# Third block's mixing: one inverse root for four layer norms, and the first two heads' tiles among the fill

## Time and profile before

| what | us |
|---|---|
| median of three runs | 3507.39 |
| lowest and highest | 3506.89, 3510.99 |
| the profiled execution: its time | 3505.32 |
| its span, first to last instruction | 3503.5 |
| TensorE busy | 3274.1 (93%) |
| VectorE, ScalarE, GpSimd busy | 1465.8, 1016.5, 1149.7 |

### The profile page before, as it was taken

How to read it: one execution, slowest core, us unless ns; L and a number is a source line. 1 busy time by engine, 2 the same in 40 slices (tenths; PEclk the granted TensorE clock), 3 DMA queues, 4 the chain that set the end, 5 groups by cost and what they waited for, 6 DMA issues and landing times.

```text
span 3503.5 us, 41394 instructions
## 1 busy us (share of the span) xinstructions
PE 3274.1 (93%) x17274; PEld 2674.5 (76%) x17274; DVE 1465.8 (42%) x3149; ACT 1016.5 (29%) x1613; POOL 1149.7 (33%) x542
## 2 busy tenths in 40 slices
PE   5988999999999998999999989999987999899999
PEld 4767888887777786877777767888765777678887
DVE  4876656453211103646765342111127666431110
ACT  2232222223222222323313332222234334322221
POOL 2312333233333342312313323444331223334443
PEclk9988999999999998998999979999988999899999
DMA  2211112112233331101101212233321112222232
GB/s 91 84 43 49 46 46 67 49 49 78 85 119 121 123 95 50 49 19 49 49 19 61 73 49 72 97 98 95 91 79 37 52 64 73 66 65 98 96 98 89
DMA packets 71482, 247.92 MB, mean 71 GB/s; under 512 B 8064, under 2 KB 8448, under 8 KB 71168
## 3 DMA queue, kind: packets, MB, share of 16 engines
q1 hardware_dynamic: 71296, 245.28, 21.9%
HBM read 243.15 MB, written 2.10 MB: 70 GB/s over the span
## 4 chain that ended last, share of the span: by engine, by line
PE 83%; DVE 12%; ACT 3%; issue 1%; POOL 1%; DMA 0%; SPq 0%; DVEq 0%; ACTq 0%
PE bank L858 21%; PE bank L860 20%; PE bank L859 20%; PE bank L898 6%; PE bank L869 3%; PE bank L1121 1%; PE bank L876 1%; PE bank L892 1%; PE bank L1306 1%; PE bank L1324 1%; PE bank L883 1%; PE bank L1315 1%; DVE t L1494 1%; PE bank L1152 1%; DVE t L1430 1%
## 5 line engine op out<-in xcount | busy, mean ns | idle before, releaser
L2533 POOL TENSOR_TENSOR R<-W,R 128x1024 fp32r<-128x1024 f32 (+2 forms) x448 | 1041.3, 2328 | 2078.4 <-ACT R L2173 2078.4
L858 PE MATMUL bank<-u,R 128*128 128x512 f32 (+1 forms) x3440 | 1399.5, 407 | 50.8 <-issue 21.7
L859 PE MATMUL bank<-u,R 128*128 128x512 f32 (+1 forms) x3440 | 1358.8, 395 | 0.0
L860 PE MATMUL bank<-u,R 128*128 128x512 f32 (+1 forms) x3440 | 1358.3, 395 | 0.0
L858 PEld LDWEIGHTS bank<-u,R 128*128 128x128 f32 (+1 forms) x3440 | 656.8, 191 | 214.1 <-issue 53.6
L860 PEld LDWEIGHTS bank<-u,R 128*128 128x128 f32 (+1 forms) x3440 | 655.1, 190 | 145.1 <-issue 1.0
L859 PEld LDWEIGHTS bank<-u,R 128*128 128x128 f32 (+1 forms) x3440 | 657.1, 191 | 130.7 <-issue 4.0
L2173 ACT ACTIVATE R<-W 128x1024 fp32r<-128x1024 f32 (+2 forms) x448 | 451.0, 1013 | 197.9 <-PE bank L860 196.2
L898 PE MATMUL bank<-t,t 128*128 128x128 f32 x2000 | 242.2, 278 | 8.5 <-DVE t L1638 4.8
L898 PEld LDWEIGHTS bank<-t,t 128*128 128x128 f32 x2000 | 235.5, 193 | 15.5 <-DVE t L1638 5.5
L2190 ACT ACTIVATE u<-t 128x512 fp32r<-128x512 f32 x126 | 76.2, 626 | 351.1 <-DVE t L1464 304.7
(11 more groups left out here) (354 smaller groups left out, 2720.6 us busy)
## 6 DMA issues: line engine op xcount, KB each, us to landing
W<-in_in SPq DMA_DIRECT2D x48, 512.0 KB, 3.5
W<-in_ff_in SPq DMA_DIRECT2D x44, 512.0 KB, 3.4
W<-in_g_qkv SPq DMA_DIRECT2D x24, 512.0 KB, 3.4
W<-in_ada SPq DMA_DIRECT2D x24, 512.0 KB, 3.4
W<-in_f1g SPq DMA_DIRECT2D x22, 512.0 KB, 3.4
W<-in_f1u SPq DMA_DIRECT2D x22, 512.0 KB, 3.4
W<-in_f2g SPq DMA_DIRECT2D x22, 512.0 KB, 3.4
W<-in_f2u SPq DMA_DIRECT2D x22, 512.0 KB, 3.5
```

The lines of the kernel that those rows point to most:

```text
L858: e.matmul(b[0:cols, :], wh, hi, start=(k == 0), stop=False)
L859: e.matmul(b[0:cols, :], wh, lo, start=False, stop=False)
L860: i = e.matmul(b[0:cols, :], wl, hi, start=False, stop=(k == KT - 1))
L2533: e.tensor_tensor(R[q % NH][:, 1024:1024 + n], W[p % NW][:, 0:n], R[q % NH][:, 0:n].bitcast(F32), SUB).then_inc(*PN.pool.up("lo", key))
```

## The change

The six tiles of heads 0 and 1 no longer stand in the order ahead of the merge but head the first fill. The MLP's chain is no longer `gn 0, gn2 0, gn 1, gn2 1, ...` but four `gn`, one new step `gnn`, then four `gn2`. `gnn` waits for all four squares and computes the four inverse roots at once, on 128x4. The planner's costs are set anew to match.

```
 SMALL
-  gm0=6, gm1=6, gm2=6, gm3=6,
+  gm=24,
 SEG
-    gn="v1.63 s.81", gn2="v5.26", gs="p.88 v1.38"
+    gn="v1.33 s.81", gnn="v2.4", gn2="v1.4", gs="p.88 v1.38"
 order()
     O += [s for j in range(4) for s in tiles("in3", 20 + j, ("gv", j), ("gvt", j))]
-    O += attention_in(("f", 0)) + attention_in(("f", 1))
-    mlp = [x for m in range(4) for x in (("gn", m), ("gn2", m))]
+    mlp = [("gn", m) for m in range(4)] + [("gnn",)] + [("gn2", m) for m in range(4)]
     for f in range(4):
         mlp += [tiles("in3", 16 + f, ("gu", f)), ("gs", f), ("pair", "yg", f)]
...
     O += merge([[s for h in range(a, 8, 2) for s in diff_head(h)] for a in range(2)] + [mlp],
-               sum([attention_in(("f", h)) for h in range(2, 8)], []), rest)
+               sum([attention_in(("f", h)) for h in range(8)], []), rest)
 VectorE
             def gn(m):
-                c, x, sq_ = small["gm%d" % m], t(G_VT[m]), t(G_T[m % 3])
+                c, x, sq_ = small["gm"][:, m:m + 1], t(G_VT[m]), t(G_T[m % 3])
...
+            def gnn():
+                c = small["gm"]
+                w.wait_ge(*GM.act.at("var", 3))
+                e.tensor_scalar(c[:, 8:12], c[:, 4:8], 1.0 / 512, 1e-5, MUL, ADD).then_inc(*GM.dve.up())
+                newton(GM.dve, c[:, 8:12], c[:, 12:16], c[:, 16:20], c[:, 20:24])
+                GM.dve.when["y",] = GM.dve.n
+
             def gn2(m):
-                c, x = small["gm%d" % m], t(G_VT[m])
-                w.wait_ge(*GM.act.at("var", m))
-                e.tensor_scalar(c[:, 2:3], c[:, 1:2], 1.0 / 512, 1e-5, MUL, ADD).then_inc(*GM.dve.up())
-                newton(GM.dve, c[:, 2:3], c[:, 3:4], c[:, 4:5], c[:, 5:6])
-                w.wait_ge(*GM.dve.now())
+                c, x = small["gm"], t(G_VT[m])
+                w.wait_ge(*GM.dve.at("y"))
                 w.wait_ge(s_l["gmlp"], 80)
-                e.scalar_tensor_tensor(out=x, in0=x, scalar=c[:, 4:5], ...
+                e.scalar_tensor_tensor(out=x, in0=x, scalar=c[:, 16 + m:17 + m], ...
```

More of the change, by code:

```diff
@@ L219 @@
 HALVES = ("ssm_conv_w", "ssm_conv_b", "gdn_conv_w", "w0", "a0", "k_a")
-SMALL = dict(nw=16, cs=8, mod=24, gc=8, hm=8, omu=17, al=1, iw=32, mx=8, lam=4, gm0=6, gm1=6, gm2=6, gm3=6, gw0=32, gw1=32,
+SMALL = dict(nw=16, cs=8, mod=24, gc=8, hm=8, omu=17, al=1, iw=32, mx=8, lam=4, gm=24, gw0=32, gw1=32,
              nb0=4, nb1=4, w80=8, w81=8, aw0=64, aw1=64, ac0=4, ac1=4)
@@ L273 @@
     ft1="s.6 v1.5", ft1s="s1.2", ft1p="p1.7", ft2="v6.5", ft2r="s.63", ft3="v1.44", gv="s.6", gu="s.6", gvt="p.44 s1.13",
-    gn="v1.63 s.81", gn2="v5.26", gs="p.88 v1.38").items()}
+    gn="v1.33 s.81", gnn="v2.4", gn2="v1.4", gs="p.88 v1.38").items()}
 HOP, SLACK, AHEAD_IN_CHAIN = 0.2, 0.3, 6
@@ L2039, in gn @@
             def gn(m):
-                c, x, sq_ = small["gm%d" % m], t(G_VT[m]), t(G_T[m % 3])
+                c, x, sq_ = small["gm"][:, m:m + 1], t(G_VT[m]), t(G_T[m % 3])
                 w.wait_ge(*GM.act.at("vt", 3))
-                e.tensor_reduce(c[:, 0:1], x, AX.X, ADD).then_inc(*GM.dve.up())
+                e.tensor_reduce(c, x, AX.X, ADD).then_inc(*GM.dve.up())
                 w.wait_ge(*GM.dve.now())
-                e.tensor_scalar(c[:, 0:1], c[:, 0:1], -1.0 / 512, None, MUL).then_inc(*GM.dve.up())
+                e.tensor_scalar(c, c, -1.0 / 512, None, MUL).then_inc(*GM.dve.up())
                 w.wait_ge(*GM.dve.now())
-                e.tensor_scalar(x, x, c[:, 0:1], None, ADD).then_inc(*GM.dve.up("c", m))
-            def gn2(m):
-                c, x = small["gm%d" % m], t(G_VT[m])
-                w.wait_ge(*GM.act.at("var", m))
-                e.tensor_scalar(c[:, 2:3], c[:, 1:2], 1.0 / 512, 1e-5, MUL, ADD).then_inc(*GM.dve.up())
-                newton(GM.dve, c[:, 2:3], c[:, 3:4], c[:, 4:5], c[:, 5:6])
-                w.wait_ge(*GM.dve.now())
+                e.tensor_scalar(x, x, c, None, ADD).then_inc(*GM.dve.up("c", m))
+            def gnn():
[4 more added lines that the diff above has]
+                GM.dve.when["y",] = GM.dve.n
+            def gn2(m):
+                c, x = small["gm"], t(G_VT[m])
+                w.wait_ge(*GM.dve.at("y"))
                 w.wait_ge(s_l["gmlp"], 80)
-                e.scalar_tensor_tensor(out=x, in0=x, scalar=c[:, 4:5], in1=t(G_LD[0]), op0=MUL, op1=MUL).then_inc(*GM.dve.up())
+                e.scalar_tensor_tensor(out=x, in0=x, scalar=c[:, 16 + m:17 + m], in1=t(G_LD[0]), op0=MUL, op1=MUL).then_inc(*GM.dve.up())
                 w.wait_ge(*GM.dve.now())
@@ L2158, in vector @@
                       r3=r3, r3b=r3b, r4=r4, rm=rm, s2=s2, s4=s4, ry1=ry1, ry2n=ry2n, ry3=ry3, an2=an2, an3=an3, sa=sa,
-                      sb=sb, dg=dg, do_=do_, gw=gw, gn=gn, gn2=gn2, gs=gs, rope=rope, lam=lam, fr=fr, ft1=ft1, ft2=ft2,
-                      ft3=ft3)
+                      sb=sb, dg=dg, do_=do_, gw=gw, gn=gn, gnn=gnn, gn2=gn2, gs=gs, rope=rope, lam=lam, fr=fr, ft1=ft1,
+                      ft2=ft2, ft3=ft3)
             for kind, *a in ORDER:
@@ L2476, in gn @@
             def gn(m):
-                c, x, sq_ = small["gm%d" % m], t(G_VT[m]), t(G_T[m % 3])
+                c, x, sq_ = small["gm"][:, 4 + m:5 + m], t(G_VT[m]), t(G_T[m % 3])
                 w.wait_ge(*GM.dve.at("c", m))
@@ L2481, in gn @@
                 w.wait_ge(*GM.pe.at("vt", 3))
-                e.activation(sq_, x, ACT.Square, accum_out=c[:, 1:2]).then_inc(*GM.act.up("var", m))
+                e.activation(sq_, x, ACT.Square, accum_out=c).then_inc(*GM.act.up("var", m))
             def gu(f):
```

## The result

The changed kernel is slower: 3513.80 us (3510.22 to 3522.54, 16 runs) against 3504.93 for the kernel before (3500.04 to 3511.05, 16 runs). The ratio is 1.0026 with a 95% interval of 1.0018 to 1.0034, so 9 us lost where 17.5 were forecast as gained, outside the stated range. A second measurement gave 1.0025 (1.0015 to 1.0035). Two slow executions, 12057.84 us of the kernel before and 4466.96 us of one of the experiments (`e7_f0_ahead`), are left out of the ratios. The profiled execution after has a span of 3509.5 us, 6.0 more than before.

A forecast was written before the change was run, and what follows sets the result against it. TensorE, busy 93% of the span, bounds the kernel; only its waits and low clock can shrink. End 18 us earlier plus 0.5 for queues gives -17.5: 3505.3 to 3487.8 profiled, 3489.9 as median; range 3475 to 3503.

The forecast's parts named there:

- The first hole goes: Start of the merge: TensorE's 20.0 us of idle time go, plus 7 us of low clock, sum 27 us.
- Norms in about 15 us, up to 9 more by meeting splits, hidden: MLP's four layer norms: chain of about 15 us, up to 9 us added by GpSimd splits, still within the slack.
- Head 1's sums near 71 to 74 us after the stage's start: Merge: head 1's tiles come last, so it starts near 2653, 1 to 3 us ahead of its chain's rhythm.
- The odd chain: Heads 1, 3, 5 and 7 in the merge: 96 us per head kept, last mark near 2943, almost unmoved.
- The tail: After head 7's sums: 59 us instead of 75 to the last matmuls, then 9.43 us until `b_proj` starts.
- The fill ends near 2977: Late in the merge: the fill's dense work ends near 2977, then the last head runs alone with short waits.
- Rival 3: Merge: head 1 comes too late, deciding from about 2660; at 2675 up to 16 us slower, 3523; chance 0.05.
- rival 2: Merge's end: odd heads set it, the last head alone hardly faster than filled; gain 3 to 6 us, 3503; chance 0.14.

The follow-up runs named there:

- e7_f0_ahead: The changed kernel with head 0's three tiles ahead of the merge again and heads 1 to 7 in the fill; ratio 0.9915 to the kernel before.

## Why the prediction was wrong

Point by point:

- *The first hole goes.* Right. From 2577 to 2655 TensorE is idle for 2.1 us, at a clock of 1.00 and 0.96. The order by hand was right too: head 0's tiles, head 1's v, the MLP's four tiles with head 0's steps between, then head 1's q and k.
- *Norms in about 15 us, up to 9 more by meeting splits, hidden.* Right: from 2577.49 to 2600.16, and TensorE waits for none of it.
- *Head 1's sums near 71 to 74 us after the stage's start.* 78.0, so I was 4 us short. TensorE ran 43 quarter tiles ahead of them where I had counted ten tiles, that is 40: three quarters of head 2's v tile came in between (3 x 1.36 = 4.1 us).
- *The odd chain at "96 us per head", "its last mark falls near 2943, almost unmoved".* This step failed. I took the pace of the earlier trace rows as a property of a head. The same matmuls in other orders gave 89 to 110 us wherever the first hole didn't lie in between. By the table, head 7's sums came at 387.6 where I had 361 to 363 (2943 less 2581): 4 of the 26 us from the start, 22 from the three paces (309.6 instead of 288).
- *The tail: 59 us and 9.43 from head 7's sums.* Measured 72.0, 3.6 more. That part of the gain is given back behind the last head was right in kind. That the sum is so near is in part luck: I had 34 us with fill and 25 without, and there were 14.4 with and 48.2 without (to 3026.12, the end of the last matmuls). By my own rates 14.4 us with fill leave 0.81 of a head, or 37 us, so the last head alone was also 11 us slower than I had it.
- *The fill ends near 2977.* Its last dense matmul is at 2977.57, which from the stage's start is 401.6 us where I had 396. But it ends 14 us behind head 7's sums where I had 34: the chain was 20 us further back in the fill than I said.

The forecast stage is 447.9 - 17.5 = 430.4 us and the measured one 459.6. The 29.2 between them are 4.0 from head 1's start, 21.6 from the three paces and 3.6 from the tail.

What is in the 7.3 us by which the paces between heads 3, 5 and 7 grew (96.2 to 103.5 in the mean), from rows of both: between the sums of heads 3, 5 and 7 there are 90 and 92 rows of the first of the three dense matmuls before, 96 and 96 after. Two such rows are a quarter tile of 1.36 us (5.44 / 4), so the order put 3.4 us more of fill beside each pair of heads. TensorE is idle for 3.8 and 2.3 us before and for 6.8 and 5.2 after, 2.9 more: the two recurring waits shown are 11.3 us of the 12.0 idle in both paces after, and 1.5 of the 6.1 before. About 1 us remains, in TensorE's busy time; the granted clock was 1.00 and 0.98 before, 0.98 and 0.98 after. But the experiments that hold fill back or shift head 1 say that more fill is not by itself the cause: 80 rows took 104.35 us, and 96 rows took 98.8 and 97.9.

The rivals named the right place. Rival 3 said that head 1 too late makes it slower; I gave it 0.05, priced it by a start at 2675 and had the threshold at 2660. The real start, 78.0 us into the stage or 2659.0 on the old trace's time, was just below that threshold, and the pace, which I held fixed in the forecast and all four rivals, did the rest. Nor do the chances fit together: rival 2's gain of 3 to 6 us lay within the 7 us that I called no change, and I counted it as faster. Of the sum, the terms inside the first 80 us held to 4 us and the one beyond was not worked out but carried over from the old order.

It could have been worked out. I followed the planner to 68 us and stopped. Its own costs, carried on, put the last `ft1p` at 415.7 against 418.5 before: hardly a gain. They also have the longer pace: the sums of heads 1, 3, 5 and 7 are planned 93.5, 94.8 and 93.6 apart in the changed kernel, those of heads 3, 5 and 7 before 88.3 and 89.5. The column "plan" goes with the stage: the four kernels planned under 390 us have the four shortest stages (421.1 at most), the next is 427.5 at 390.3. Above 400 it sorts only roughly, with the order that puts head 2 beside head 1, the one with only head 1 late and the kernel before itself out of place. In the kernel before the stage is 29 us above its plan and in the changed kernel 44; that the planned costs of the old norms (5.26 for a `gn2` of 4.1) overstated the hole is one reason, argued and not tried.

What was not settled: why an order with the chains half a pace apart gives 98 us in one kernel and 104 in another with as much fill. Of the 5.1 us between them 3.3 are TensorE's idle time, and the two recurring waits are there in the slower one only; that they are the cause was not tried by taking them away.

## What to carry to other kernels

When a hand-made or planned order changes, a spacing read from the old trace can't be carried over: here it was 96 us before and 89 to 110 in the other orders, the first hole aside. Work the new order out to its end, chain by chain, before summing. Two changes that each help (9 and 21 us here) can lose together when a scheduler turns the first into a new priority: a cheaper step fell due sooner, and its followers were placed ahead of the tiles that the longest chain waited for. With two dependent chains and a stock of filling work, ask which chain ends last and when it starts. Here one condition that held four tiles back for that chain turned 9 us lost into 30 gained.

## What the runs showed of the hardware

- Kernels with the same instructions ahead of the stage reach it at different times: 2575.7 to 2587.2 us over the fourteen profiled executions. The changed kernel did so at 2575.99 and 2575.70 in two. Where it comes from was not looked into; it is as large as the effect studied, so stages were compared, and medians of runs beside each other.
- A small VectorE instruction of 0.17 us takes 2.3 where a GpSimd split of 2.4 us starts in the same moment (2.20; 2.28, 2.32 after). It cost nothing beside the norms and 1.1 us on TensorE per head in the middle. The Trainium skill, "SBUF — State Buffer", section "SBUF: two separate sides", says that a vector instruction with two SBUF inputs and a GpSimd one lock each other out for a whole instruction. The trace agrees for the root's steps: they start just behind the split and end with it. Two TENSOR_SCALARs with one input met a split too, one of 128x4 at 2586.19 (1.38 us, others of 128x4 take 0.17) and one of 128x512 at 2581.02 (2.34 us for 0.49). The section names instructions in a 2-port mode as well; whether these ran in one no run here shows.
- A tail without fill is slow twice: in the last 55.5 us the mean granted clock was 0.57, and the last L1352 pair took 2.08 us (the same shape takes 1.02 right behind the fill, as L1347 at 2979.55). The Trainium skill, "TensorE: Matmul & The Clock Gate", section "Part 1: The HAM clock gate", speaks of an idle engine at half clock; the trace agrees so far as the engine stood still for 33.9 of the 55.5 us, in waits of up to 9.43.
